# The end of a fused diffusion block: the last norm and residual taken with tokens on partitions

## The reference, cut to what matters

```python
h = rmsnorm(x, g_ffn_pre[l]) * (1.0 + sc_f) + sh_f
x = x + gt_f * rmsnorm(swiglu(h, ffn_w_gu[l], ffn_w_down[l]), g_ffn_post[l])

def rmsnorm(x, g):
    xf = x.astype(jnp.float32)
    y = xf * lax.rsqrt(jnp.mean(xf * xf, axis=-1, keepdims=True) + RMS_EPS)
    return (y * g.astype(jnp.float32)).astype(x.dtype)

def swiglu(h, w_gu, w_down):
    g, u = jnp.split(h @ w_gu, 2, axis=-1)
    return (jax.nn.silu(g) * u) @ w_down
```

## Time and profile before

| what | value |
|---|---|
| median of 3 runs | 1537.72 us (1537.6 to 1542.82) |
| the profiled execution, its own time | 1543.49 us |
| span of its trace, first to last instruction | 1541.7 us |
| granted TensorE clock, mean | 0.964 |
| TensorE busy (matmul) | 1429.8 us, 93% |
| VectorE, ScalarE, GpSimd busy | 743.7, 540.9, 617.3 us |
| share of the chain that ended last: TensorE, VectorE, ScalarE | 78%, 12%, 3% |

### The profile page before, as it was taken

How to read it: one execution, slowest core, us unless ns; L and a number is a source line. 1 busy time by engine, 2 the same in 40 slices (tenths; PEclk the granted TensorE clock), 3 DMA queues, 4 the chain that set the end, 5 groups by cost and what they waited for, 6 DMA issues and landing times.

```text
span 1541.7 us, 20500 instructions
## 1 busy us (share of the span) xinstructions
PE 1429.8 (93%) x7699; PEld 1163.0 (75%) x7699; DVE 743.7 (48%) x1036; ACT 540.9 (35%) x845; POOL 617.3 (40%) x285
## 2 busy tenths in 40 slices
PE   4899999989998999899899999999998999999994
PEld 1388677879986777678677888878877888877883
DVE  5563647892845778537874111133356111111235
ACT  3662553312314667634332222232222222321220
POOL 1552112361336444174334444444443444444440
PEclk9799999999999999999999999999999999999996
DMA  8752101413113444432422333323323433332321
GB/s 322 257 179 75 42 28 31 134 37 113 50 33 97 122 117 118 136 110 84 135 69 82 95 95 95 96 88 99 99 82 113 119 95 98 93 104 77 102 85 54
DMA packets 236697, 156.54 MB, mean 102 GB/s; under 512 B 11043, under 2 KB 222385, under 8 KB 236507
## 3 DMA queue, kind: packets, MB, share of 16 engines
q1 hardware_dynamic: 234629, 148.70, 31.8%
q10 hardware_dynamic: 2006, 7.00, 1.3%
HBM read 147.25 MB, written 8.81 MB: 101 GB/s over the span
## 4 chain that ended last, share of the span: by engine, by line
PE 78%; DVE 12%; ACT 3%; POOL 3%; issue 2%; DMA 1%; SPq 1%; ACTq 0%; DVEq 0%
PE ps L1786 32%; PE ps L1791 16%; PE ps L1944 10%; PE ps L1947 5%; PE ps L2100 2%; POOL w_lo L1071 1%; PE ps L2066 1%; PE ps L2077 1%; DVE a_f L1640 1%; PE ps L1960 1%; DVE a_f L1678 1%; PE ps L1835 1%; DVE pr L1622 1%; DVE x L1679 1%; PE ps L1841 1%
## 5 line engine op out<-in xcount | busy, mean ns | idle before, releaser
L1055 POOL TENSOR_TENSOR w_lo<-raw,w_hi 128x1024 fp32r<-128x1024 f32 x152 | 371.6, 2445 | 466.5 <-ACT w_hi L668 466.5
L1786 PE MATMUL ps<-hb_hi,w_hi 128*128 128x512 f32 x832 | 328.9, 395 | 22.8 <-DVE g_t L1707 12.2
L1786 PE MATMUL ps<-hb_lo,w_hi 128*128 128x512 f32 x832 | 327.0, 393 | 0.0
L668 ACT ACTIVATE w_hi<-raw 128x1024 fp32r<-128x1024 f32 x152 | 160.0, 1053 | 186.8 <-PE ps L1791 179.4
L1791 PE MATMUL ps<-hb_hi,w_lo 128*128 128x512 f32 x832 | 207.9, 392 | 1.9 <-POOL w_lo L1055 1.9
L1786 PEld LDWEIGHTS ps<-hb_hi,w_hi 128*128 128x128 f32 x832 | 158.2, 190 | 59.6 <-DVE g_t L1707 13.3
L1071 POOL TENSOR_TENSOR w_lo<-raw,w_hi 128x1024 fp32r<-128x1024 f32 x22 | 96.1, 4369 | 232.3 <-ACT w_hi L823 232.3
L1791 PEld LDWEIGHTS ps<-hb_hi,w_lo 128*128 128x128 f32 x832 | 156.6, 188 | 36.7 <-POOL w_lo L1055 2.3
L1786 PEld LDWEIGHTS ps<-hb_lo,w_hi 128*128 128x128 f32 x832 | 158.3, 190 | 32.5
L1944 PE MATMUL ps<-ha_hi,w_hi 128*128 128x512 f32 (+2 forms) x432 | 164.7, 381 | 3.7 <-ACT w_hi L823 3.3
L1944 PE MATMUL ps<-ha_lo,w_hi 128*128 128x512 f32 (+2 forms) x432 | 162.0, 375 | 0.0
(11 more groups left out here) (247 smaller groups left out, 2059.2 us busy)
## 6 DMA issues: line engine op xcount, KB each, us to landing
raw<-in_ffn_w_gu SPq DMA_DIRECT2D x88, 512.0 KB, 3.8
ada1x<-in_ada_w SPq DMA_DIRECT2D x32, 512.0 KB, 4.0
raw<-in_ffn_w_down SPq DMA_DIRECT2D x32, 512.0 KB, 4.0
raw<-in_w_in SPq DMA_DIRECT2D x22, 512.0 KB, 4.0
ada<-in_ada_w SPq DMA_DIRECT2D x4, 2048.0 KB, 22.8
raw<-in_w_out SPq DMA_DIRECT2D x16, 512.0 KB, 4.0
raw<-in_ffn_w_down SPq DMA_DIRECT2D x16, 384.0 KB, 3.3
raw<-in_ktab SPq DMA_DIRECT2D x8, 512.0 KB, 7.2
```

The lines of the kernel that those rows point to most:

```text
L668: act.activation(w_hi[:, b, :], raw[:, b, :], ACT.Copy).then_inc(hi_done, 1)
L1055: pool.tensor_tensor(w_lo[:, b, :], raw[:, b, :], w_hi[:, b, :].bitcast(F32), ALU.subtract).then_inc(lo_done, 1)
L1786: pe.matmul(dst, w_hi[:, b, k * P:(k + 1) * P], x, start=start and k == 0 and n == 0, stop=False)
```

## The change

For the second half only, the last norm and residual are computed with tokens on partitions.

- During the down phase TensorE transposes x1 (32 transposes, `x1_columns`; two pieces before job 0, two after job 2) and ScalarE copies each 128 x 1024 piece to x1t.
- After each k ScalarE, in place of VectorE, squares the bank (into nrm for k = 0, else sq) and copies it, multiplied by gffn, to ydg; VectorE adds sq to nrm. After the jobs of tile k TensorE transposes ydg of tile k - 1 (`down_columns`, 4 transposes) into banks 4 to 7. VectorE copies the first four tiles' banks to yta once tile 3 has been turned.
- The sum over features is four matmuls with a slice of nrm as stationary operand and one column of ones, so each token's sum lands on its partition: 128 x 4. The eps, root and reciprocal act on 128 x 4.
- The output is formed by eight scalar_tensor_tensor (times rstd4, plus x1t), 128 x 512 each, into ost; each second one raises `o_ev`, and SyncE sends the four DMAs in order 0, 1, 2, 3. The copies L1774 and L1047 and the chain above are gone.
- VectorE's wait for the first half's output DMAs (`st_out`) stands behind the down phase instead of ahead of it. For h = 1 TensorE's and ScalarE's down loops are written out instead of being hardware loops.

The diff, without the semaphore declarations:

```diff
--- before.py
+++ after.py
@@ -255,6 +255,9 @@
         yacc = at("yacc", S_ + 6144, [HALF])
         x1sq = at("x1sq", H_ + 16384, [KT, HALF])
         ost = at("ost", S_ + 32768, [4, D])
+        x1t = at("x1t", H_, [4, D])
+        yta = at("yta", H_ + 16384, [4, HALF])
+        ydg = at("ydg", H_ + 24576, [2, HALF])
 
         a_hi = at("a_hi", P_HY, [FT, HALF], F32R)
         a_lo = at("a_lo", P_HY + 45056, [FT, HALF], F32R)
@@ -294,6 +297,8 @@
         ninv = small("ninv", [4])
         lam = small("lam", [8, 4])
         hbias = small("hbias", [8])
+        var4 = small("var4", [4])
+        rstd4 = small("rstd4", [4])
         amin = small("amin", [2, 2])
         asum = small("asum", [2, 2])
         arec = small("arec", [2, 2])
...
@@ -651,8 +656,8 @@
                                 w_dn[:, c * KT:c * KT + nk, ds((i * 2 + q // 3) * P, P)], nk)
                 if h == 0:
                     pair0(J0 + DOWN_JOBS, src_g)
-            for q, done, n in ((0, o_ev, 5), (2, o_ea, 1), (1, o_ev, 6), (3, o_ea, 2)):
-                sp.wait_ge(done, n)
+            for q in range(4):
+                sp.wait_ge(o_ev, 5 + q)
                 sp.dma_start(out[0, (4 + q) * P:(5 + q) * P, :], ost[:, q, :]).then_inc(st_out[q % 2], 16)
             for b in range(2):
                 sp.wait_ge(st_out[b], 64)
@@ -1036,15 +1041,34 @@
                             if q % 3 == 1:
                                 h2_heads(1, range(2 * i + q // 3, 2 * i + q // 3 + 1))
                 else:
-                    with act.Fori(0, 3) as i:
-                        for q in range(6):
-                            split(i * 6 + (J0 + q + 1), i * 3 + (J0 // 2 + (q + 1) // 2), (q + 1) % 2)
-                    for q in range(5):
-                        head_of(18 + J0 + q + 1)
-            root(5)
-            for q in range(2, 4):
-                act.wait_ge(o_tp, 4 + q + 1)
-                act.activation(ost[:, q, :], ps[:, 2 * q:2 * q + 2, :].rearrange("p a b -> p (a b)"), ACT.Copy).then_inc(o_ea, 1)
+                    def x1_columns(q):
+
+                        act.wait_ge(t_tp, q + 1)
+                        act.activation(x1t[:, q, :], ps[:, 4 + 2 * (q % 2):6 + 2 * (q % 2), :].rearrange("p a b -> p (a b)"), ACT.Copy).then_inc(t_ev, 1)
+
+                    def down_out(k):
+
+                        act.wait_ge(job_done, J0 + 3 * k + 3)
+                        if k >= 3:
+                            act.wait_ge(y_add, k - 2)
+                        act.activation(sq[:, k % 2, :] if k else nrm[:], ps[:, 2 + k % 2, :], ACT.Square).then_inc(y_sq, 1)
+                        if k >= 2:
+                            act.wait_ge(t_tp, 4 + k - 1)
+                        act.activation(ydg[:, k % 2, :], ps[:, 2 + k % 2, :], ACT.Copy, scale=gffn[:, k:k + 1]).then_inc(dn_free, 1)
+
+                    for j in range(23):
+                        head_of(J0 + j + 1)
+                        if j == 0:
+                            x1_columns(0)
+                            x1_columns(1)
+                        if j % 3 == 0 and j:
+                            down_out(j // 3 - 1)
+                        if j == 3:
+                            x1_columns(2)
+                            x1_columns(3)
+                    down_out(7)
+            act.wait_ge(n_var, 6)
+            act.activation(var4[:], var4[:], ACT.Sqrt).then_inc(n_sqrt, 1)
 
 
         @block.gpsimd
@@ -1754,24 +1778,34 @@
                 J0 += GU_JOBS
                 if h == 0:
                     rstd_of(3)
+                    for k in range(KT):
+                        ffn_input(1, k)
+                        dve.wait_ge(job_done, J0 + 3 * k + 3)
+                        dve.tensor_scalar(yd[:, k, :], ps[:, 2 + k % 2, :], 1.0, None, ALU.mult).then_inc(dn_free, 1)
+                        dve.wait_ge(dn_free, 8 * h + k + 3)
+                        add_square(yd[:, k, :], k, nrm, a_f)
+                        ffn_rest(1, k)
                 else:
-                    for b in range(2):
-                        dve.wait_ge(st_out[b], 32)
-                for k in range(KT):
-                    if h == 0:
-                        ffn_input(1, k)
-                    dve.wait_ge(job_done, J0 + 3 * k + 3)
-                    dve.tensor_scalar(yd[:, k, :], ps[:, 2 + k % 2, :], 1.0, None, ALU.mult).then_inc(dn_free, 1)
-                    dve.wait_ge(dn_free, 8 * h + k + 3)
-                    add_square(yd[:, k, :], k, nrm, a_f)
-                    if h == 0:
-                        ffn_rest(1, k)
+                    for k in range(1, KT):
+                        dve.wait_ge(y_sq, k + 1)
+                        link(dve.tensor_tensor(nrm[:], nrm[:], sq[:, k % 2, :], ALU.add))
+                        dve.nop().then_inc(y_add, 1)
+                        if k == 4:
+                            dve.wait_ge(t_tp, 8)
+                            for q in range(4):
+                                dve.tensor_copy(yta[:, q, :], ps[:, 4 + q, :]).then_inc(t_ev, 1)
                 dve.nop().then_inc(n_sum, 1)
-            rstd_of(5)
-            add_ffn(1, range(KT))
-            for q in range(2):
-                dve.wait_ge(o_tp, 4 + q + 1)
-                dve.tensor_copy(ost[:, q, :], ps[:, 2 * q:2 * q + 2, :].rearrange("p a b -> p (a b)")).then_inc(o_ev, 1)
+            dve.wait_ge(n_ps, 6)
+            dve.tensor_scalar(var4[:], ps[:, 0, 0:4], 1.0 / D, EPS, ALU.mult, ALU.add).then_inc(n_var, 1)
+            for b in range(2):
+                dve.wait_ge(st_out[b], 32)
+            dve.wait_ge(t_ev, 8)
+            dve.wait_ge(n_sqrt, 6)
+            link(dve.reciprocal(rstd4[:], var4[:]))
+            for q in range(4):
+                dve.scalar_tensor_tensor(ost[:, q, 0:HALF], yta[:, q, :], rstd4[:, q:q + 1], x1t[:, q, 0:HALF], ALU.mult, ALU.add)
+                dve.scalar_tensor_tensor(ost[:, q, HALF:D], ps[:, 4 + q, :], rstd4[:, q:q + 1], x1t[:, q, HALF:D],
+                                         ALU.mult, ALU.add).then_inc(o_ev, 1)
 
 
         @block.tensor
@@ -2192,23 +2226,52 @@
                     sum_over_features(3, nrm)
                     pe.wait_ge(n_x1, 16)
                 pe.wait_ge(g_al, FT * (h + 1))
-                with pe.Fori(0, 4) as i:
-                    for q in range(6):
-                        f, c = q // 3, q % 3
-                        nk = KT if c < 2 else FT - 2 * KT
-                        if c == 0:
-                            pe.wait_ge(dn_free, i * 2 + (8 * h + f + 1))
-                        product(i * 6 + (J0 + q), q % 2, ps[:, 2 + f, :],
-                                lambda k: (a_hi[:, c * KT + k, :], a_lo[:, c * KT + k, :]), nk, start=c == 0, stop=c == 2)
-            pe.wait_ge(o_ev, 4)
-            sum_over_features(5, nrm)
-            for k in range(KT):
-                pe.wait_ge(n_fin, k + 2)
-                for q in range(4):
-                    ins = pe.transpose(ps[:, 2 * q + k // 4, (k % 4) * P:(k % 4 + 1) * P],
-                                       x1[:, k, HALF + q * P:HALF + (q + 1) * P], ident[:])
-                    if k == KT - 1:
-                        ins.then_inc(o_tp, 1)
+                def down_job(i, q):
+
+                    f, c = q // 3, q % 3
+                    nk = KT if c < 2 else FT - 2 * KT
+                    if c == 0:
+                        pe.wait_ge(dn_free, i * 2 + (8 * h + f + 1))
+                    product(i * 6 + (J0 + q), q % 2, ps[:, 2 + f, :],
+                            lambda k: (a_hi[:, c * KT + k, :], a_lo[:, c * KT + k, :]), nk, start=c == 0, stop=c == 2)
+
+                def x1_columns(q):
+
+                    for k in range(KT):
+                        ins = pe.transpose(ps[:, 4 + 2 * (q % 2) + k // 4, (k % 4) * P:(k % 4 + 1) * P],
+                                           x1[:, k, HALF + q * P:HALF + (q + 1) * P], ident[:])
+                    ins.then_inc(t_tp, 1)
+
+                def down_columns(k):
+
+                    pe.wait_ge(dn_free, 8 + k + 3)
+                    for q in range(4):
+                        ins = pe.transpose(ps[:, 4 + q, (k % 4) * P:(k % 4 + 1) * P], ydg[:, k % 2, q * P:(q + 1) * P], ident[:])
+                    ins.then_inc(t_tp, 1)
+
+                if h == 0:
+                    with pe.Fori(0, 4) as i:
+                        for q in range(6):
+                            down_job(i, q)
+                else:
+                    pe.wait_ge(o_ev, 4)
+                    x1_columns(0)
+                    x1_columns(1)
+                    for k in range(KT):
+                        for c in range(3):
+                            down_job(k // 2, 3 * (k % 2) + c)
+                        if k == 0:
+                            pe.wait_ge(t_ev, 2)
+                            x1_columns(2)
+                            x1_columns(3)
+                        else:
+                            pe.wait_ge(t_ev, 4 if k < 5 else 8)
+                            down_columns(k - 1)
```

(13 more changed lines are left out.)

## The result

The changed kernel took 1527.3 us in the median of 4 runs (1526.44 to 1527.95), the kernel before beside it 1540.0 (4 runs, 1537.6 to 1542.82): ratio 0.9916, 95% interval 0.9893 to 0.994. That is 12.9 us less by the ratio (9 to 16 by its interval) and 12.7 by the medians. Forecast were 11.6 us less and 1526.1 us. The span of the profiled execution went from 1541.7 to 1525.0 us, which is 16.7 us and thus more than the runs show; where the surplus comes from is taken up under e1.

What follows compares the result with a forecast made beforehand. TensorE bounds the down phase; behind it VectorE carries nearly all of a 31.06 us tail. Terms -17.8 (tail), +6.3 (transposes), -0.1 (joint) give -11.6 us, so 1537.7 becomes 1526.1 us; range 1521 to 1533.

Steps and rivals of the forecast that it cites:

- The tail: From last down product to end of span: 31.06 us would become 13.3, so 17.8 us go.
- The first output operation: In the tail, after square, transposes, sum and narrow norm: would start 3.9 us behind the last product.
- The eight output operations: VectorE at the end: 0.75 from SBUF, 0.69 from PSUM, 0.03 between, 6.0 us in all.
- the 0.3 set aside for chained waits: In the tail: an allowance of 0.3 us for chained waits not counted one by one.
- TensorE's share: Ahead of the end of the last product: 56 added transposes would cost TensorE 6.3 us.
- 0.113 per transpose: On TensorE: us per added transpose, from 16 taking 1.91 us in the first half's output.
- The rival at 0.272: In the down phase: transposes don't overlap and cost 0.272 us each, 15.2 in all, total 1535.0; chance 0.08.
- The joint: From gate/up to down: idle gap and 1.9 us clock loss remain, transposes start 0.1 to 0.3 earlier; gain 0.1 us.
- The clock did not fall behind any group of transposes: Rival at nine down-phase joints: clock falls after each transpose group, 1.9 us each, total 1543.2 if all; chance 0.04.
- drain behind the load: Rival in the tail: root waits for its table plus a 1.38 us drain, +0.8 us, total 1526.9; chance 0.05.
- never 4.8: Rival at the end: last output DMA lands in 4.8 us, not 2.6, +2.2 us, total 1528.3; chance 0.15.
- upper level of the runs: In the measured median: part of 0.05 taken off the chance of faster, for a median on that level; runs spread 5 us.

Runs made afterwards that it cites:

- e1: Kernel before, with only TensorE's and ScalarE's down loops of the second half written out; ratio 0.9999 to the kernel before.
- e2: Changed kernel with the old wide 128x512 norm chain added ahead of the narrow one, its result unused; ratio 0.994 to the kernel before, tail 18.81 us.
- e3: Changed kernel with each output operation split into a multiplication and an addition, 16 in place of 8; ratio 0.9927 to the kernel before, tail 16.68 us.
- e4: Changed kernel with 4 instead of 32 transposes of x1, output incomplete; ratio 0.9897 to the kernel before, down phase 127.42 us.
- e9: Changed kernel with last squares summed separately by TensorE, joined on 128x4, root table loaded early, transposes awaited later; ratio 0.9906 to the kernel before, tail 11.48 us.
- e11: Changed kernel run again unaltered; median 1532.1 us, ratio 0.9924 to the kernel before.
- e5: Changed kernel with the first 16 x1 transposes issued ahead of TensorE's wait for a_lo; ratio 0.9894 to the kernel before, down phase 127.19 us.
- e7: Changed kernel with the last tile's squares added by TensorE instead of VectorE and the root's table loaded early; ratio 0.9895 to the kernel before, tail 12.18 us.

## Why the prediction was right

**The tail: 19.1 us less, forecast 17.8.** The mechanism held line by line, with most sizes a little high. The first output operation starts at 3.47 us behind the last product (forecast 3.9): ScalarE starts after 0.02 and not 0.15, and its square and scaled copy follow each other at 0.60 and 0.59, since the two overlap (the copy starts at 1513.52, before the square ends, and is 0.68 long by itself). The last four transposes went the other way, 0.66 and not 0.45. The eight output operations follow each other at 0.66 and not at 0.75 and 0.69 plus 0.03, which is 5.4 us and not 6.0. The end is 3.14 us behind the last operation (1521.86), forecast 3.17. Thus 0.4 us came from the start and 0.6 from the pace, and the 0.3 set aside for chained waits was not needed: that makes the 1.3 us.

**Which part of the tail's gain is whose.** Both chains can be cut at the same four events. From the last product to the start of the sum over features it is 2.4 us before and 1.9 after. The norm, from there to the first output operation, takes 6.9 and 1.6. The output operations (the eight pairs of `add_ffn`, 1519.94 to 1532.83, and the eight operations, 1516.48 to 1521.86) take 12.9 and 5.4. From the last of them to the end of the span it is 8.9 and 3.1. So the norm gives 5.3 us, the output operations 7.5, and the transposes and copies that no longer stand behind them, with transfers that start earlier, 5.7. By e2 the wide norm would cost 5.75 us by itself and 1.08 through the clock. The eight operations also do the work of the copies; by e3, output in two operations would give back 4.7.

**TensorE's share: +6.1, forecast +6.2.** The one number that mattered most, 0.113 per transpose, was 0.109 to 0.110: 1.75 for 16 and 0.44 for 4, and 0.109 by e4. The sixteen products behind a group of 4 take 3.66 to 3.68 us and not 3.63, so such a group costs 0.48 in all. Against e1, which has the written-out loops too, the stage grew by 6.4 us, which is 0.114 for each of the 56; the 0.3 us of the loops is what makes 6.1 of it. There is no idle time ahead of any group, nor a late bank at the start of a tile. The rival at 0.272 needed -7.6 in e4 and got -3.0.

**The joint.** As forecast the dip in the clock stayed and cost the same: 16 transposes at 2.54 against 1.75, and the first sixteen matmuls at 4.70 against 3.63, 1.9 in all, as before. The start was 0.3 earlier (idle 2.47 us and not 2.75), at the top of the 0.1 to 0.3 that I gave it, but not for my reason: I thought of the split, for which the transposes don't wait. In e1 the first product does wait for it and still starts 2.47 us behind gate/up, so this 0.3 comes with the written-out loops, by the rows TensorE's. I had counted them as costing and giving nothing.

**The rivals.** The clock did not fall behind any group of transposes inside the phase: each period with a group of 4 is 15.43 to 15.47 us, the products' 14.96 plus 0.48, and no more. The table load for the root ran from 1514.22 to 1515.50 directly behind the copy, and the root began at 1515.93, 0.02 us behind VectorE's eps. So there was no drain behind the load as described in the Trainium skill, "ScalarE: Activation LUTs", section "What ACT_TABLE_LOAD costs". With its 1.38 us on top of the load the root could not have started before 1516.88, an estimate from that page, and the trace does not agree with it. The transfers landed in 2.6 to 2.7 us each, never 4.8. They do carry the same pace as VectorE now (1.32 us per piece, 1.3 us per 512 KB). So an earlier start still pays, as in e9; that a faster VectorE at that point would not is my inference, and no run tests it.

**What the prediction missed, and where luck helped.** It read a span that happened to be 3.7 us longer ahead of the change than the next one. It noticed that the profiled execution lay 5.8 us above the median and applied its difference to the median, which is why that surplus did not mislead it. The total of 1526.1 against 1527.3 looks closer than its base was: the kernel before came out at 1540.0 beside the change and not at 1537.7, so 1528.4 would have followed from the same difference. The difference was 1.1 to 1.3 us too small, the base 2.3 too low, and the two partly cancelled. That the runs gave 12.9 is itself no finer than some us either way; the stages carry the argument. The allowance for the "upper level of the runs" was a guess at two levels; the runs of the kernel before beside e1 and e11 are spread over 12 and 14 us without a gap between two levels.

## What to carry to other kernels

Where one engine has no idle time and the others wait at the end, work moved from the tail into the stream costs its issue pace on that engine (here 0.109 us a transpose, 0.114 with what it costs at the joints). Find the pace in a gapless run of the same operation, not in the duration of one. Choose the layout of the last stage by what must be replicated: with tokens on partitions the norm's eps, root and reciprocal act on 4 columns instead of 512, and scale and residual merge into one operation. Put such added work into an idle gap if there is one: in e5 the 16 transposes in the gap lost their own cost of 1.8 us, and 1.5 of the 1.9 that the fall of the clock had cost went with it.

## What the runs showed of the hardware

- The clock is worth as much as the edit. In the changed kernel 2.5 us of idle time at the joint are followed by a granted clock of 0.56 to 0.58 from 1386 to 1390, and 1.9 us are lost; with 0.75 us idle it stayed at 1.00 (e5). Totals of one and the same kernel lay up to 14 us apart beside e9 to e11 (1537.41 us at a mean clock of 0.966, 1551.28 at 0.958). That half-clock stretches make all of this is inferred from the mean clocks and a few windows.
- Transposes kept the clock up like matmuls: e5's 16 transposes were all that filled the gap, and the granted clock was 1.00 in the windows from 1384 to 1392.
- A one-column fp32 matmul is two instructions of 0.10 to 0.12 us each (0.80 for eight in the changed kernel, 0.79 and 0.91 in e9). Sixteen in a row (e7) were 1.9 us, 1.1 more than eight, and the VectorE add that they replaced was 0.69.
- VectorE multiplies 128x512 by a per-partition number in 0.41 us of the chain when it reads SBUF but in 0.67 when it reads PSUM (e3; 0.48 and 0.74 as durations). The form with two tensors takes 0.66 from either (changed kernel).
